# Where the modulation panels of a two-block transformer kernel are computed: fewer lent to GpSimd, more placed in the delta rule and the routing, and one square moved

## The chip, the cores and the metric

One Trainium2 chip, one of its cores. The metric is the device time of one launch in microseconds (us); lower is better. Engines are named as in the profile: PE is TensorE (PEld its weight loads), DVE VectorE, ACT ScalarE, POOL GpSimd, SP SyncE, which here only issues the transfers of weights.

## The reference

256 tokens of width 1024 go through two blocks, all in float32.

```python
# first block, two layers
h = h + mix(rmsnorm(h))              # layer 0: attention + pooling; layer 1: spatial gating + gated delta rule
h = h + memory_cross_attention(rmsnorm(h), mem_n, wq, wkv, wo)
h = h + conv_ffn(rmsnorm(h))
# second block, two layers
mod = silu(c) @ ada_w[l] + ada_b[l]  # 1024 x 6144, one row
sh_m, sc_m, g_m, sh_f, sc_f, g_f = split(mod, 6)
x = x + g_m * (four_attentions(rmsnorm(x) * (1 + sc_m) + sh_m) @ w_out[l])
x = x + g_f * ffn(rmsnorm(x) * (1 + sc_f) + sh_f)   # layer 0 swiglu, layer 1 eight experts, top 2
```

`c` is an input, so `mod` depends on nothing else that the kernel computes. One of the four attentions of the second block is the difference attention, whose output is normalised by head (`o * rsqrt(mean(o*o))`).

## The kernel before

Weights arrive as panels of 1 MB (128 x 2048 floats), in one fixed order, in a ring of six slots. SP loads panel n into slot n % 6 once panel n - 6 is released. All engines run their own program, written out by hand, and meet at semaphores; each does its instructions strictly in the order of the program.

The order of the stages, with the names in the code: mix0 (attention "moba", pooling, output projection), xat0 (first cross attention), ffn0, mix1 (spatial gating and delta rule), xat1 (second cross attention), ffn1, mix2 (attentions "s0"), ffn2, mix3 (attentions "s1"), ffn3 (routing, then the experts). Each stage begins with `transpose_norm`, in which PE turns the normalised tokens; before that PE has to wait for the norm on DVE and ACT.

The `mod` of both layers needs 48 panels of `ada_w` (2 layers x 6 parts x 4 quarters, `ADA_ORDER`). Each is done in one of two ways:

- **on PE, at a hook.** `ada(hook, n)` does n panels with eight matmuls of 128x256 each against the conditioning vector spread over 128 columns (`COND`), L1036. `ADA_AT` says how many at which hook; a hook with a stage's name stands at the start of `transpose_norm`. DVE reads the result in its own `ada(hook)`: a gate part (2 or 5) in one operation, L2258, the others in three, L2261 to L2267. 17 panels before.
- **lent to POOL.** For a name in `LENT_AHEAD` the panel of `ada_w` is put in the ring ahead of the named weight panel. POOL multiplies it by the conditioning vector and adds it up to 128x256 (`sum_lent`, L2664 to L2670), in one of three buffers `LENTS`; only then is the ring slot free. PE adds the 128 partitions with a few small matmuls (`take`, L577, or L574 for a gate part) and frees the buffer; DVE adds the result (`taken`, L2285 or L2282). POOL starts a stage's panels when that stage's norm is there, and panel i waits until panel i - 3 is taken. `TAKE_LATER` says after which step of a cross attention how many are taken and into which PSUM bank. 31 panels before: 2 in mix0 (taken in xat0), 10 in xat0, 11 in mix1, 8 in xat1.

A cross attention (`cross`) is: four query panels `xq`, in layer 0 the key panels `xk` 0 and 1 (7 us of PE each), then `attention`: step s computes the scores of unit s (four units), a panel `xv` beside it, the turned probabilities of unit s - 2 and the mixing of unit s - 3. Between scores and turned probabilities DVE scales the scores, finds the maxima (L1923, L1929), ACT takes the exponential (L1463) and DVE scales the result in place (L1941). The last steps, s = 4 to 6, have no panel beside them. Then follows `project`, four panels `xattn_wo`.

In mix1 PE inverts a matrix in five levels (`lv` 1 to 5) with one panel beside each, then scans four chunks; at the end it waits for DVE's last norm (`delta_out`) before `turn_outputs` and `project`.

In mix2 and mix3 the difference attention is the first of the four. `keep` on ACT copies the mixed result of a group out of PSUM (L1410) and, for the difference attention, squares it right after (L1517, `diff_squares`). PE uses the squares in `diff_sums` (L711), which stands after the whole `attention`; the scale that comes of them is needed at the last of the four output panels (`diff_spread`, L721).

In ffn3 PE computes the router's logits (L889), turns the tokens back (L897) while DVE picks the two best experts, then the places (L905), and gathers the first expert's tokens (L917) before the loop over the experts begins (L947).

Of the kernel before, what the change touches and what calls it, by code (L numbers as in the profile page):

```python
# [27 lines left out]
ACT = mybir.ActivationFunctionType  # L28
# [101 lines left out]
def build_program(nc, d, out):  # L130

    with ExitStack() as ctx:
# [34 lines left out]
        with ExitStack() as over_it:  # L167
# [5 lines left out]
            OT = under("OT", KD, T)  # L173
# [312 lines left out]
        def moe_unit(what, it, c):  # L486
# [9 lines left out]
        ADA_AT = {"xat0": 1, "ffn0": 1, "mix1": 1, "xat1": 1, "ffn1": 1, "mix2": 4,  # L496
                  "ffn2": 3, "mix3": 3, "ffn3": 2}

        LENT_AHEAD = {"mix0": (("out", "mix0", 0), ("out", "mix0", 2)),  # L500
                      "xat0": tuple(("xq", 0, j) for j in range(4)) + (("xk", 0, 0), ("xk", 0, 1)) + tuple(("xv", 0, j) for j in range(4)),
                      "mix1": tuple(("qkv", j) for j in range(6)) + (("u", 0), ("u", 1), ("vz", 0), ("vz", 1), ("gate", 0)),
# [3 lines left out]
        TAKE_LATER = {"xat0": {("xq", 1): (2, 4), ("xq", 3): (1, 5), ("xk", 0): (1, 6), ("xk", 1): (1, 7),  # L506
                               0: (1, 7), 1: (1, 6), 2: (1, 7), 3: (1, 6), 4: (1, 7), 5: (1, 6), 6: (1, 7)},
# [22 lines left out]
        def _(pe):  # L530
# [351 lines left out]
            def experts():  # L882
# [16 lines left out]

                ps = claim("places")  # L900
# [249 lines left out]
            for lv in range(1, len(LEVELS)):  # L1150
                if lv == 1:
                    panel_tok(("vz", 1))
                elif lv < 4:
                    panel_tok(("gate", lv - 2))
                else:
                    panel_T(("xk", 1, lv - 4), rhs=MT)
                if lv > 1:
                    take(("mix1", lv + 2), 1)
                pe.wait_ge(sem("level_ready"), lv)
                for tb in range(NT):  # L1160
                    products(("y", lv), M_of(gM), M_of(gX), tb)
                wait_read((("y", lv), 0), (("y", lv), 1))
                if lv < len(LEVELS) - 1:
                    for tb in range(NT):
                        products(("z", lv), M_of(gXT), M_of(gY), tb)
                for tb in range(NT):
                    products(("zt", lv), M_of(gY), M_of(gXT), tb)
                if lv == 4:
                    pe.wait_ge(sem("vn_ready"), 1)
                    for j in range(2):  # L1170
                        ps = claim(("sgu", j))
                        for c in range(2):
                            for tb in range(NT):
                                g = 2 * j + c
                                m = nc.tensor.matmul(ps[:, c * T + tb * P:c * T + tb * P + P],
                                                     VG[:, tb, g * P:g * P + P], WST[:, g, :], start=True, stop=True)
                        filled(m, ("sgu", j))
# [9 lines left out]
            for n in range(4):  # L1187
# [29 lines left out]
                filled(m, ("so", n))  # L1217
            pe.wait_ge(sem("delta_out"), 1)
# [188 lines left out]
        def _(act):  # L1407
# [98 lines left out]
            def keep(key, u):  # L1506
# [8 lines left out]
                if u["turns"] == 2:  # L1515
                    wait_drained(act, name)
                    nc.scalar.activation(DSQ, dst, ACT.Square).then_inc(sem("diff_squares"), 1)  # L1517
# [275 lines left out]
            for layer in range(2):  # L1793
# [39 lines left out]
                attention(k2)  # L1833
                act.wait_ge(sem("diff_mean"), layer + 1)
# [17 lines left out]
        def _(dve):  # L1852
# [272 lines left out]
            def experts():  # L2125
# [87 lines left out]
                tokens_low(0, base[2], base[3])  # L2213
                rounds = expert_rounds(dve)
# [220 lines left out]
            for lv in range(1, len(LEVELS)):  # L2435
# [41 lines left out]
                if lv > 1:  # L2477
                    taken(("mix1", lv + 2))
# [17 lines left out]
            for n in range(4):  # L2496
# [32 lines left out]
                .then_inc(sem("delta_out"), 1)  # L2529
            evac(("ot", "mix1", 1), OT[:, 6:8, :])  # L2530
# [108 lines left out]
        def _(pool):  # L2639
# [62 lines left out]
            sum_lent("mix0")  # L2702
# [220 lines left out]
```

## Time and profile before

| | us |
|---|---|
| median of 3 runs | 2716.41 (2714.31 to 2717.51) |
| the profiled execution, its own time | 2719.55 |
| its span in the profile, first to last instruction | 2717.7 |
| PE busy | 2619.8 (96%) |
| DVE busy | 1726.9 (64%) |
| ACT busy | 1309.5 (48%) |
| POOL busy | 301.7 (11%) |
| mean granted clock of TensorE | 0.984 of 2.4 GHz |

### The profile page before, as it was taken

To read this page: it belongs to the slowest core of one execution; us is meant where nothing else is said; L and a number is where in the kernel's file an instruction comes from. 1 tells how busy PE (TensorE), PEld (TensorE's weight loads), DVE (VectorE), ACT (ScalarE), POOL (GpSimd) and SP (SyncE) were. 2 spreads that over 40 slices of the span, in tenths; PEclk is the share of its full clock that TensorE was granted. 3 is DMA by queue.
4 is the path that set the end of the run, shared out by engine and by line. 5 is a ranking of instruction groups with operands and counts; after the bars stand their busy time and mean duration, and the time that the engine had idled before them with its cause. 6 is when DMAs were issued, how large, how long until landed. Compare 5 with 4: busy or idle time off the path is not lost.

```text
span 2717.7 us, 39002 instructions
## 1 busy us (share of the span) xinstructions
PE 2619.8 (96%) x13620; PEld 2171.0 (80%) x13620; DVE 1726.9 (64%) x2535; ACT 1309.5 (48%) x1931; POOL 301.7 (11%) x288
## 2 busy tenths in 40 slices
PE   7999999999899999999999998999999999999998
PEld 7677898887587998767998775888888888887886
DVE  1312776662226773555553553989898989889897
ACT  2211544411124442243332242777777777777776
POOL 0465000860360000000000000000000000000000
PEclk9999999999899999999999998999999999999999
DMA  7345544441355445315444303989898989898997
GB/s 318 124 182 214 209 185 160 186 179 68 135 205 194 186 185 180 106 35 201 186 185 164 107 33 118 359 322 383 319 381 328 375 329 374 322 366 336 349 365 277
DMA packets 87635, 627.29 MB, mean 231 GB/s; under 512 B 9760, under 2 KB 9920, under 8 KB 12800
## 3 DMA queue, kind: packets, MB, share of 16 engines
q1 hardware_dynamic: 84512, 613.45, 59.7%
q0 software_dynamic: 2480, 11.31, 1.1%
q8 instruction: 57, 0.93, 0.1%
q10 hardware_dynamic: 560, 1.38, 0.1%
q14 instruction: 26, 0.21, 0.0%
HBM read 625.06 MB, written 1.05 MB: 230 GB/s over the span
## 4 chain that ended last, share of the span: by engine, by line
PE 93%; DVE 3%; ACT 2%; issue 1%; POOL 1%; DMA 0%; DVEq 0%; SPq 0%; ACTq 0%; POOLq 0%
PE bank L947 23%; PE bank L838 14%; PE bank L975 11%; PE bank L606 11%; PE bank L852 7%; PE bank L619 6%; PE bank L791 6%; PE bank L655 2%; PE bank L693 2%; PE bank L1075 1%; PE bank L1036 1%; PE bank L990 1%; PE bank L917 1%; PE bank L962 1%; PE bank L679 1%
## 5 line engine op out<-in xcount | busy, mean ns | idle before, releaser
L1410 ACT ACTIVATE sb_parts<-sb_ring 128x1024 fp32r<-128x1024 f32 x873 | 873.0, 1053 | 125.0 <-PE bank L975 38.6
L2155 DVE TENSOR_TENSOR sb_parts<-sb_ring,sb_parts 128x1024 fp32r<-128x1024 f32 x675 | 786.9, 1218 | 10.8 <-ACT sb_parts L1410 10.8
L947 PE MATMUL bank<-sb_parts 128*128 128x512 f32 x2688 | 661.5, 396 | 2.5 <-DVE sb_parts L2147 1.8
L947 PEld LDWEIGHTS bank<-sb_parts 128*128 128x128 f32 x2688 | 494.9, 188 | 113.5 <-issue 9.4
L838 PE MATMUL bank<-sb_parts 128*128 128x256 f32 x3168 | 387.3, 284 | 7.1 <-DVE sb_XT L2080 5.8
L838 PEld LDWEIGHTS bank<-sb_parts 128*128 128x128 f32 x3168 | 386.1, 193 | 9.9 <-issue 7.7
L975 PE MATMUL bank<-sb_parts 128*128 128x512 f32 x1344 | 323.8, 390 | 0.0
L975 PEld LDWEIGHTS bank<-sb_parts 128*128 128x128 f32 x1344 | 251.7, 188 | 52.1
L606 PE MATMUL bank<-sb_XT,sb_ring 128*128 128x256 f32 x1152 | 259.7, 385 | 7.0 <-DVE sb_XT L1902 3.9
L2057 DVE TENSOR_TENSOR sb_parts<-sb_ring,sb_parts 128x1024 fp32r<-128x1024 f32 x198 | 232.8, 1220 | 34.3 <-ACT sb_parts L1410 34.3
L606 PEld LDWEIGHTS bank<-sb_XT,sb_ring 128*128 128x128 f32 x1152 | 219.6, 193 | 42.2 <-issue 12.7
L1410 ACT ACTIVATE sb_REG<-bank 128x512 f32<-128x512 f32 (+2 forms) x119 | 67.1, 574 | 338.7 <-PE bank L606 197.6
L852 PE MATMUL bank<-sb_parts 128*128 128x512 f32 x792 | 185.3, 390 | 0.0
L791 PE MATMUL bank<-sb_ring,sb_OT 128*128 128x512 f32 x384 | 168.9, 600 | 3.3 <-DVE sb_OT L1966 1.7
L852 PEld LDWEIGHTS bank<-sb_parts 128*128 128x128 f32 x792 | 146.6, 188 | 29.5 <-DVE sb_parts L2057 0.3
L2664 POOL TENSOR_TENSOR sb_ring<-sb_ring,sb_small 128x512 f32<-128x512 f32 x124 | 131.4, 1091 | 196.7 <-DVE sb_XH L1887 164.2
L791 PEld LDWEIGHTS bank<-sb_ring,sb_OT 128*128 128x128 f32 x384 | 73.2, 192 | 94.0 <-issue 90.9
L1463 ACT ACTIVATE sb_REG<-sb_REG,sb_small 128x256 f32<-128x256 f32 x112 | 56.0, 500 | 144.1 <-DVE sb_small L1929 144.1
L619 PE MATMUL bank<-sb_ring,sb_XT 128*128 128x256 f32 (+1 forms) x512 | 116.4, 389 | 4.2 <-ACT sb_O L1806 4.2
L619 PEld LDWEIGHTS bank<-sb_ring,sb_XT 128*128 128x128 f32 x512 | 98.3, 201 | 19.7 <-issue 6.6
L1410 ACT ACTIVATE sb_parts<-bank 128x256 fp32r<-128x256 f32 (+1 forms) x130 | 52.8, 413 | 121.7 <-PE bank L962 112.2
L1427 ACT ACTIVATE sb_XH<-sb_H 128x1024 f32<-128x1024 f32 x24 | 25.2, 1049 | 160.5 <-DVE sb_H L2030 100.2
(345 smaller groups left out, 2379.7 us busy)
## 6 DMA issues: line engine op xcount, KB each, us to landing
sb_ring<-in_moe_panels SPq DMA_DIRECT2D x342, 1024.0 KB, 4.9
sb_ring<-in_ada_w SPq DMA_DIRECT2D x48, 1024.0 KB, 4.8
sb_ring<-in_ffn_w_up SPq DMA_DIRECT2D x44, 1024.0 KB, 4.9
sb_ring<-in_ffn_w SPq DMA_DIRECT2D x33, 1024.0 KB, 4.8
sb_ring<-in_w_in SPq DMA_DIRECT2D x26, 1024.0 KB, 4.8
sb_ring<-in_ffn_w_down SPq DMA_DIRECT2D x22, 1024.0 KB, 6.6
sb_ring<-in_xattn_wkv SPq DMA_DIRECT2D x16, 1024.0 KB, 6.9
sb_ring<-in_od_w_in SPq DMA_DIRECT2D x12, 1024.0 KB, 5.6
```

The lines of the kernel that those rows point to most:

```text
L606: m = nc.tensor.matmul(ps[:, c * T:c * T + T], wt[:, k, c * P:c * P + P], rhs[:, k, :], start=k == 0, stop=k == KD - 1)
L619: m = nc.tensor.matmul(ps[:, tb * T:tb * T + w], lhs[:, k, tb * P:tb * P + P], wt[:, k, 0:w], start=k == 0, stop=k == KD - 1)
L791: m = nc.tensor.matmul(acc[j][:, :], OT[:, 2 * pair + c, j // 2 * P:j // 2 * P + P], wt[:, c, j % 2 * 512:j % 2 * 512 + 512], start=kk == ...
L838: m = nc.tensor.matmul(banks[b][:, half * T:half * T + T], w[:, kk, :], x[:, kk, :], start=t == 0, stop=t == len(terms) - 1)
L852: m = nc.tensor.matmul(banks[4 + j][:, :], h[:, g, tb], w[u][:, half], start=start and c == 0 and t == 0, stop=stop and c == 1 and t == 2, ...
L947: m = nc.tensor.matmul(banks[par][:, :], x[:, k, :], w[:, cols], start=k == 0 and t == 0, stop=k == KD - 1 and t == 2, skip_group_check=True)
L975: m = nc.tensor.matmul(banks[4 + j][:, :], h[:, par, c, :], w[:, cols], start=start and c == 0 and t == 0, stop=stop and c == 1 and t == 2 ...
L1410: return nc.scalar.activation(out, in_, ACT.Copy)
L1463: m = nc.scalar.activation(PR[:, g % 3, j, :], SS[:, g % 2, j, :], ACT.Exp, bias=NM[:, 2 * (g % 4) + j:2 * (g % 4) + j + 1], accum_out=RS[ ...
L2057: V_.tensor_tensor(as_panel(LOW[u], what), half_panel(n, what, c, it), as_panel(HIGH[u], what), ALU.subtract).then_inc(sem("low_ready"), 1)
L2155: V_.tensor_tensor(LOW[u], ring[slot][:, 1024 * c:1024 * c + 1024], HIGH[u], ALU.subtract) \
L2664: m = G.tensor_tensor(w[:, k:k + 2, :], w[:, k:k + 2, :], c[:, k:k + 2, :], ALU.mult)
```

## The change

It changes which of the 48 modulation panels are computed where, and where one square stands:

- `LENT_AHEAD`: the 2 lent panels of mix0 are gone, xat0 has 7 in place of 10, mix1 has 12 in place of 11. So 27 are lent, and 21 are done on PE.
- `TAKE_LATER["xat0"]`: 7 takes of one panel each, after `xq` 3, `xk` 0 and steps 0, 1, 3, 5, 6, in place of 12 panels taken after `xq` 1 (two), `xq` 3, `xk` 0, `xk` 1 and steps 0 to 6.
- mix1 takes one panel at every level, the first included.
- `ADA_AT`: a new hook "delta" with 2 panels, before PE's wait for `delta_out`; a new hook "route" with 3 panels, between the turned tokens and PE's wait for the chosen experts; ffn3 has 1 in place of 2.
- The square of the difference attention moves from the middle of ACT's attention to its end.

As `ADA_ORDER` is fixed, every hook and every take after the first works on other parts than before.

```diff
-        ADA_AT = {"xat0": 1, "ffn0": 1, "mix1": 1, "xat1": 1, "ffn1": 1, "mix2": 4,
-                  "ffn2": 3, "mix3": 3, "ffn3": 2}
+        ADA_AT = {"xat0": 1, "ffn0": 1, "mix1": 1, "delta": 2, "xat1": 1, "ffn1": 1, "mix2": 4,
+                  "ffn2": 3, "mix3": 3, "ffn3": 1, "route": 3}
-        LENT_AHEAD = {"mix0": (("out", "mix0", 0), ("out", "mix0", 2)),
-                      "xat0": tuple(("xq", 0, j) for j in range(4)) + (("xk", 0, 0), ("xk", 0, 1)) + tuple(("xv", 0, j) for j in range(4)),
-                      "mix1": tuple(("qkv", j) for j in range(6)) + (("u", 0), ("u", 1), ("vz", 0), ("vz", 1), ("gate", 0)),
+        LENT_AHEAD = {"xat0": (("xq", 0, 0), ("xq", 0, 1), ("xq", 0, 3), ("xk", 0, 0), ("xv", 0, 0), ("xv", 0, 1), ("xv", 0, 3)),
+                      "mix1": tuple(("qkv", j) for j in range(6)) + (("u", 0), ("u", 1), ("vz", 0), ("vz", 1), ("gate", 0), ("gate", 1)),
-        TAKE_LATER = {"xat0": {("xq", 1): (2, 4), ("xq", 3): (1, 5), ("xk", 0): (1, 6), ("xk", 1): (1, 7),
-                               0: (1, 7), 1: (1, 6), 2: (1, 7), 3: (1, 6), 4: (1, 7), 5: (1, 6), 6: (1, 7)},
+        TAKE_LATER = {"xat0": {("xq", 3): (1, 4), ("xk", 0): (1, 5), 0: (1, 7), 1: (1, 6), 3: (1, 6), 5: (1, 7), 6: (1, 6)},
...
# tensor, experts(), after the turned tokens
+                ada("route", ADA_AT["route"])
                 ps = claim("places")
                 pe.wait_ge(sem("experts_chosen"), 1)
...
# tensor, the levels of mix1 (vector: the same with taken)
-                if lv > 1:
-                    take(("mix1", lv + 2), 1)
+                take(("mix1", "lv", lv), 1)
...
# tensor, after the scan
+            ada("delta", ADA_AT["delta"])
             pe.wait_ge(sem("delta_out"), 1)
...
# scalar, keep()
-                if u["turns"] == 2:
-                    wait_drained(act, name)
-                    nc.scalar.activation(DSQ, dst, ACT.Square).then_inc(sem("diff_squares"), 1)
...
# scalar, mix2 and mix3
                 attention(k2)
+                wait_drained(act, ("mixed", k2, 0))
+                nc.scalar.activation(DSQ, OT[:, 0:2, :], ACT.Square).then_inc(sem("diff_squares"), 1)
...
# vector, experts(), after the first tokens_low
+                ada("route")
...
# vector, after delta_out
+            ada("delta")
             evac(("ot", "mix1", 1), OT[:, 6:8, :])
...
# gpsimd
-            sum_lent("mix0")
             sum_lent("xat0")
```

## Rows read from the trace of the kernel before

**Rows 1.** The page, busy time, share of the span and instructions, PE to POOL
```profile
PE 2619.8 (96%) x13620; PEld 2171.0 (80%) x13620; DVE 1726.9 (64%) x2535; ACT 1309.5 (48%) x1931; POOL 301.7 (11%) x288
```

**Rows 2.** Timeline, end of attention in mix0: start us, us, instruction [idle before]
```profile
102.86 1.13 PE L655 MATMUL bank<-sb_REG 64*128 64x256 f32 x4
102.88 2.36 DVE L1941 TENSOR_SCALAR sb_REG<-sb_REG,sb_small 128x256 f32<-128x256 f32 x2
...
105.39 0.63 PE L679 MATMUL bank<-sb_CST,sb_REG 128*128 128x128 f32 x4 [1.40 <-DVE sb_REG L1941]
...
112.70 1.99 PE L1059 MATMUL bank<-sb_REG 128*128 128x256 f32 x8
```

**Rows 3.** Timeline, end of the attentions in mix2, PE, DVE and ACT
```profile
1198.23 1.13 PE L655 MATMUL bank<-sb_REG 64*128 64x256 f32 x4
1198.26 0.61 DVE L1941 TENSOR_SCALAR sb_REG<-sb_REG,sb_small 128x256 f32<-128x256 f32 x2
...
1205.85 1.95 PE L711 MATMUL bank<-sb_CST,sb_XH 128*128 128x1 f32 x16
1205.96 0.60 ACT L1410 ACTIVATE sb_OT<-bank 128x512 f32<-128x512 f32 x1 [1.18 <-PE bank L693]
...
1207.66 4.54 PE L791 MATMUL bank<-sb_ring,sb_OT 128*128 128x512 f32 x10
```

**Rows 4.** Timeline of PE in the first cross attention
```profile
165.22 14.06 PE L606 MATMUL bank<-sb_XT,sb_ring 128*128 128x256 f32 x64
...
181.52 8.74 PE L606 MATMUL bank<-sb_MT,sb_ring 128*128 128x256 f32 x32 [1.90 <-DMA sb_ring<-in_xattn_wkv]
...
207.52 0.50 PE L577 MATMUL bank<-sb_CST,sb_LENTS 128*128 128x1 f32 x4
...
241.53 0.63 PE L679 MATMUL bank<-sb_CST,sb_REG 128*128 128x128 f32 x4 [0.87 <-DVE sb_REG L1941]
...
247.16 0.58 PE L577 MATMUL bank<-sb_CST,sb_LENTS 128*128 128x1 f32 x4 [0.99 <-POOL sb_LENTS L2670]
```

**Rows 5.** Timeline of POOL there: the last operation of two lent panels in succession
```profile
173.54 0.72 POOL L2670 TENSOR_TENSOR sb_LENTS<-sb_ring 128x256 f32<-128x256 f32 x1
...
182.24 0.72 POOL L2670 TENSOR_TENSOR sb_LENTS<-sb_ring 128x256 f32<-128x256 f32 x1
```

**Rows 6.** Timeline of PE at the end of the delta rule
```profile
686.17 1.97 PE L769 MATMUL bank<-sb_CST,sb_O 128*128 128x128 f32 x8 [7.49 <-DVE sb_O L2528]
688.97 16.55 PE L791 MATMUL bank<-sb_ring,sb_OT 128*128 128x512 f32 x33 [0.83 <-issue]
...
718.67 3.62 PE L1036 MATMUL bank<-sb_ring,sb_COND 128*128 128x256 f32 x16
```

**Rows 7.** Windows: stretch, us, busy PE, PEld, DVE, ACT, POOL, granted clock, DMA share, GB/s
```profile
686.10:693.00 6.90, 6.00 (x13) 3.42 (x14) 0.71 (x2) 0.60 (x1) 0.00 (x0) 0.50 0.00 0
...
1669.50:1690.00 20.50, 15.26 (x72) 14.82 (x72) 10.50 (x39) 5.70 (x9) 0.00 (x0) 0.50 0.04 9
```

**Rows 8.** Timeline of ACT in the attentions of mix2, the square
```profile
1181.77 0.63 ACT L1517 ACTIVATE sb_XH<-sb_OT 128x512 f32<-128x512 f32 x1
```

**Rows 9.** Timeline of PE, with one row of DVE, from the norm of ffn3 to the experts' loop
```profile
1657.44 7.07 PE L1036 MATMUL bank<-sb_ring,sb_COND 128*128 128x256 f32 x32
1665.03 1.97 PE L633 MATMUL bank<-sb_CST,sb_XH 128*128 128x128 f32 x16 [0.51 <-DVE sb_XH L1887]
...
1668.05 0.75 DVE L2258 TENSOR_TENSOR sb_GATE<-bank,sb_GATE 128x256 f32<-128x256 f32 x2
...
1674.38 3.65 PE L897 MATMUL bank<-sb_CST,sb_XT 128*128 128x128 f32 x16
1679.77 2.27 PE L905 MATMUL bank<-sb_REG,sb_CST 128*128 128x9 f32 x10 [1.73 <-DVE sb_REG L2631]
1685.55 5.93 PE L917 MATMUL bank<-sb_REG,sb_XH 128*128 128x128 f32 x32 [3.51 <-DVE sb_REG L2137]
1693.25 3.03 PE L947 MATMUL bank<-sb_parts 128*128 128x512 f32 x12 [1.77 <-DVE sb_parts L2147]
```

More of the change, by code:

```diff
@@ L2476, in _ @@
                         step(V_.tensor_tensor(u_, tmp, u_, ALU.mult))
-                if lv > 1:
-                    taken(("mix1", lv + 2))
+                taken(("mix1", "lv", lv))
                 evac((("y", lv), 1), flat(gY)[:, 512:1024], bank_of((("y", lv), 1))[:, :])
```

## The prediction, made before the changed kernel was run

> **What bounds the kernel now.** I read the page first. PE is busy for 2619.8 us of a span of 2717.7, so it sets the time almost everywhere [rows 1]. A change can then do three things: give PE less or more to do, fill or open one of its waits (97.9 us in all), or move its granted clock, whose mean is 0.984. The list of PE's waits says where the waits are, and the largest single one behind something other than a norm at a stage's start is that at the end of the delta rule. Then I read the timeline at each place that the diff touches, and there the reader is to look at the gap in brackets and at the duration of the row behind it: a row twice as long as its like ran at 1.2 GHz. The windows say so directly [rows 7]. The experts' loop, the last 1020 us, is not touched and has no waits of PE; it only starts earlier or later.
>
> **Prices.** A modulation panel on PE costs 3.62 us as one and 7.07 as two in a row, so about 3.6 each [rows 6, 9]. A lent one costs PE a take, a row of 0.50 of which the next matmul overlaps some: 0.4 [rows 4]. POOL needs 8.7 us for it (182.24 less 173.54) [rows 5]. Four panels more on PE are thus 14.4 us of work, against 1.6 of takes saved. Everything hangs on which waits they fall into.
>
> **End of attention in mix0.** The two lent panels go. POOL summed the second one beside DVE's scaling L1941, which took 2.36 us for two, where the same pair takes 0.61 with POOL idle [rows 2, 3]. PE waits 1.40 for it and then runs some rows at half clock. From the last scores to the end of the mixing it is 112.70 - 102.86 = 9.84 us here, and 1205.85 - 1198.23 = 7.62 in mix2, where the same steps run without POOL [rows 2, 3]. I take the whole difference: -2.2 (bounds 0, if the two stages differ for another reason, and -2.4). The Trainium skill (SBUF — State Buffer, SBUF: two separate sides) says that VectorE and GpSimd take turns at a shared pair of ports, each for a whole instruction; by that rule the wait goes with POOL's work, which the trace bears out with 2.36 against 0.61.
>
> **First cross attention (xat0).** Five takes fewer are 2.0, of which one after `xk` 1 now covers a wait for the same panel's copy: -1.6. The wait of 1.90 for the weights of `xk` 0 is one for a ring slot that POOL held: before, it had two panels of mix0 to be taken first and then four in five panels. A weight panel is 14.06 / 2 = 7.03 us of PE [rows 4], so POOL at 8.7 fell behind. In the new order there is no lent panel before `xq` 2 and only one between `xq` 3 and `xk` 1, and POOL's third is done at 173.4, before PE reaches the first take: -1.9. The panel behind that wait took 8.74, where its like take 7.0 to 7.15, at half clock in part: -1.6. Then POOL: its fourth panel starts with the take at 178.7, the last of its seven ends near 221, while PE has 20 us of steps left. So the last steps have no POOL beside them; the wait of 0.87 for L1941 goes (2.36 becomes 0.61) and the 0.99 for the last `LENTS` too [rows 4]: -1.9. Laid out step by step PE reaches the output projection near 240.6, and 248.0 before. Sum -7.0, by the layout -7.4; I take -7.2 (bounds -4.5, if the takes and the DVE wait give nothing, and -8). The ring is late nowhere: the longest hold is the fourth lent panel until 187.8, and the panel loaded in its slot (`xv` 1) is wanted at 205.
>
> **mix1, levels.** One take more on PE at level 1, where PE did not wait: +0.4. POOL's twelfth panel runs in levels 1 and 2 beside DVE: 0 to +1.1 more. +0.4.
>
> **Delta rule.** Two panels, 7.07 to 7.24, go into a wait of 7.49 [rows 6], so they are done just before `delta_out`. DVE adds them behind that (0.75 for two, [rows 9]) while PE turns the outputs: nothing. If DVE were late there, it would be by 0.8. More comes from the clock: after the wait PE ran at half until 693.0 [rows 7]; 8 transposes took 1.97, where 16 take the same in ffn3 [rows 6, 9], so 1.0 is lost there, and of 4.0 us of projection half, 2.0. With PE busy all the way the clock has no reason to fall: -3.0 (bounds 0, if the panels do not hold it, and -3.3).
>
> **The square.** In the middle of ACT's attention nobody waited for it (0.63, [rows 8]) and PE had no gap there, so taking it away gives 0. At the end PE waits: before, L711 started at 1205.85; now ACT first copies the last group (until 1206.56), then squares for 0.63, and L711 starts at 1207.3 [rows 3, 8]. The projection is behind L711 in PE's program, though its first panel needs nothing of it. +1.45 in mix2 and in mix3, 2.9. A new gap can also bring the clock down; if it does, that costs up to 3.0 each (6.9 us at 0.50 with 6.0 busy, [rows 7]). I take +0.5 each on average: +3.9 (bounds 2.9 and 8.9).
>
> **ffn3 and the routing.** Before, two panels (7.07) covered the norm but for 0.51 [rows 9]. One of them leaves a wait of 4.0: no gain, and with the half clock beginning a little earlier +0.8. The three panels stand between the turned tokens, which end at 1678.0, and a wait of 1.73. They are 10.7, and the clock is at half there (1669.5 to 1690.0, [rows 7]), so some 1.2 more until it rises. Behind them all is in series: places, DVE's slots (3.51), gather, split (1.77), and nothing of it can start earlier. Given back: the wait of 1.73; the places, 2.27 at half clock, 1.1; the gather, 5.93, of which a clock at full would give back 2.3, but the wait of 3.51 comes before it: 1.4. Sum 0.8 + 10.7 + 1.2 - 1.7 - 1.1 - 1.4 = +8.5 (bounds +6, all at full clock, and +12, nothing given back). The ring has the experts' first three panels by then, and the other three come before the gather ends.
>
> The Trainium skill (TensorE: Matmul & The Clock Gate, Part 1: The HAM clock gate) says that half rate is the default and activity lifts it. By that rule the three panels would lift it before the places, the lower bound of +6; it also speaks against the 4.0 us left open before the transposes of ffn3 and against the square's gap.
>
> **Sum.** -2.2 - 7.2 + 0.4 - 3.0 + 3.9 + 8.5 = +0.4. The profiled execution took 2719.55 by its own time (1.85 more than its span), 3.1 above the median of 2716.41. So 2719.95 for a like execution, and 2716.8 as a median. What a measurement can tell from no change is some 0.2%, 5.4 us: faster is below 2711.0, slower above 2721.8.
>
> **The rivals.**
> - *The routing is cheap.* The panels lift the clock within the first of them and it stays: +6 there, and the square opens no clock loss, +2.9. Then -2.2 - 7.4 + 0.4 - 3.0 + 2.9 + 6 = -3.3, and with one of the half-clock stretches elsewhere falling away (3.0, as above) -6.3: 2710. For: 15.26 busy in 20.5 us at half is 7.6 lost, a large sum to win back. Against: the wait of 3.51 stays. Chance 0.25, half of which is past the bound.
> - *Slower: the clock falls at the new gaps.* The 4.0 in ffn3, the 3.5 before the gather and the two squares' gaps lie between gaps after which rows ran at half (7.49 and 1.90 did it, [rows 4, 6]) and those that left the clock alone (0.51, [rows 9]). Routing +11, squares +6: sum +5.0 or more, 2722. It decides once the squares and the gather all run at half. Chance 0.2.
> - *Spacing does nothing.* POOL is as late as before, as its wait is for the takes: xat0 gives only the five takes and the part in mix0, so +0.4 + 5.6 = +6.0, 2722. Against: the layout leaves POOL 20 us. Chance 0.05.
> - *The panels in the delta rule are late* (a slot is not loaded): +3.6 there, 2720, within the forecast.
>
> **How the numbers follow.** The forecast, 2711 to 2722, has 0.5 of the chance. The range for 8 in 10 adds the most of the first two rivals: 2709 to 2723. Faster: 0.12 from the first rival and 0.13 from a forecast whose routing or square I have too dear: 0.25. Slower: 0.2. Same: 0.55.
>
> **What would show it.** PE's wait at L769 under 0.5 and the granted clock at 1.00 over 680 to 705; no DMA wait in xat0 and its projection 9 to 10 us earlier than before (with mix0's part); L711 with a wait of 1.4 behind ACT's square; three panels at L1036 in the routing and the experts' loop starting some 8 later after the norm of ffn3 than before. It is wrong if the places do not wait for the panels, if POOL is still late in xat0, or if the clock's stretches at half outside these places change by more than two.

## The result, and the profile after

| | before | after |
|---|---|---|
| median of the runs | 2717.49 (2714.31 to 2719.84, 8 runs) | 2724.34 (2721.96 to 2726.92, 8 runs) |
| ratio, 95% interval | | 1.0024 [1.0013, 1.0035] |
| span of the profiled execution | 2717.7 | 2722.7 |
| PE busy; mean granted clock | 2619.8; 0.984 | 2631.9; 0.986 |

The change makes the kernel slower: by the medians 6.85 us, by the ratio 6.5 (3.5 to 9.5), where the forecast was +0.4. At 2724.34 it lies 2 us above the upper rival's place (2722) and 1.3 above the range's end of 2723. Of the 7.5 us between the forecast of 2716.8 and the result, 1.1 is the kernel before, whose median was 2716.41 in the three runs at hand then and 2717.49 in eight. The experts' loop takes 1024.5 us to the end in both profiles, so all of it is decided ahead of it.

The page of the kernel after, first part; its line answers to [rows 1]: 12 us more of PE and 32 POOL instructions fewer (the 4 panels).

```profile
PE 2631.9 (97%) x13680; PEld 2182.4 (80%) x13680; DVE 1720.3 (63%) x2531; ACT 1308.7 (48%) x1931; POOL 267.9 (10%) x256
```

Timeline of the kernel after, end of attention in mix0, PE and DVE. It answers to [rows 2]: the scaling takes 0.62 where it took 2.36, PE's wait of 1.40 is one of 0.72, and from the last scores to the end of the mixing it is 112.52 - 104.79 = 7.73 in place of 9.84.

```profile
104.79 1.13 PE L653 MATMUL bank<-sb_REG 64*128 64x256 f32 x4
...
107.48 0.61 DVE L1939 TENSOR_SCALAR sb_REG<-sb_REG,sb_small 128x256 f32<-128x256 f32 x2
108.24 0.63 PE L677 MATMUL bank<-sb_CST,sb_REG 128*128 128x128 f32 x4 [0.72 <-DVE sb_REG L1939]
...
112.52 1.99 PE L1058 MATMUL bank<-sb_REG 128*128 128x256 f32 x8
```

Timeline of PE after, first cross attention. It answers to [rows 4]: both key panels take 7.15, no row waits for a transfer, and the output projection starts 240.09 - 147.08 = 93.01 behind the norm's transposes, where it was 248.03 - 147.25 = 100.78. One wait has grown, from 0.86 to 1.20, ahead of the scores of the first step; in this whole stage the granted clock is 1.00 (windows 180 to 194, 194 to 200 and 200 to 240). It will matter for the lesson.

```profile
185.74 7.15 PE L604 MATMUL bank<-sb_MT,sb_ring 128*128 128x256 f32 x32
...
194.09 1.96 PE L653 MATMUL bank<-sb_REG 128*128 128x256 f32 x8 [1.20 <-DVE sb_REG L1862]
...
240.09 2.41 PE L789 MATMUL bank<-sb_ring,sb_OT 128*128 128x512 f32 x5 [0.25 <-DVE sb_MODC L2284]
```

Timeline of DVE in the same stage, all four pairs of the scaling. POOL's last operation there ends at 221.33: the two pairs that it worked beside took 2.28 each, the two after it 0.62.

```profile
206.69 2.28 DVE L1939 TENSOR_SCALAR sb_REG<-sb_REG,sb_small 128x256 f32<-128x256 f32 x2
215.77 2.28 DVE L1939 TENSOR_SCALAR sb_REG<-sb_REG,sb_small 128x256 f32<-128x256 f32 x2
224.84 0.62 DVE L1939 TENSOR_SCALAR sb_REG<-sb_REG,sb_small 128x256 f32<-128x256 f32 x2
233.66 0.62 DVE L1939 TENSOR_SCALAR sb_REG<-sb_REG,sb_small 128x256 f32<-128x256 f32 x2
```

Timeline of PE after, from the last chunks of the levels to the end of the delta rule's projection. It answers to [rows 6]: the two panels stand where the wait of 7.49 was, and the projection takes 27.70, where it took 29.86. Its first row is new: a wait for a PSUM bank, of which more below.

```profile
639.23 7.14 PE L604 MATMUL bank<-sb_MT,sb_ring 128*128 128x256 f32 x32 [0.87 <-DVE sb_REG L1862]
...
672.55 8.36 PE L1035 MATMUL bank<-sb_ring,sb_COND 128*128 128x256 f32 x32
680.75 1.04 PE L767 MATMUL bank<-sb_CST,sb_O 128*128 128x128 f32 x8
682.62 27.70 PE L789 MATMUL bank<-sb_ring,sb_OT 128*128 128x512 f32 x64 [0.83 <-DVE sb_OT L1862]
710.16 3.62 PE L1035 MATMUL bank<-sb_ring,sb_COND 128*128 128x256 f32 x16
```

Timeline of PE and ACT after, the square's new place in mix2. It answers to [rows 3, 8]: ACT's copy ends at 1198.14, the square follows, and PE stands for 1.20. The 48 rows behind it take 22.54.

```profile
1198.04 0.62 ACT L1831 ACTIVATE sb_XH<-sb_OT 128x512 f32<-128x512 f32 x1
1198.71 1.95 PE L709 MATMUL bank<-sb_CST,sb_XH 128*128 128x1 f32 x16 [1.20 <-ACT sb_XH L1831]
1200.52 22.54 PE L789 MATMUL bank<-sb_ring,sb_OT 128*128 128x512 f32 x48
1222.90 1.05 PE L719 MATMUL bank<-sb_CST,sb_XH 128*128 128x128 f32 x8
```

Timeline of PE after, from the norm of ffn3 to the experts' loop. It answers to [rows 9], and a reader should add up from the first row to the last: 1698.20 - 1651.73 = 46.47, where it was 1693.25 - 1657.44 = 35.81.

```profile
1651.73 3.62 PE L1035 MATMUL bank<-sb_ring,sb_COND 128*128 128x256 f32 x16
1659.32 3.68 PE L631 MATMUL bank<-sb_CST,sb_XH 128*128 128x128 f32 x16 [3.97 <-DVE sb_XH L1885]
1664.39 6.96 PE L887 MATMUL bank<-sb_WR,sb_XT 128*128 128x8 f32 x32 [1.40 <-DVE sb_XT L1903]
1671.21 3.65 PE L895 MATMUL bank<-sb_CST,sb_XT 128*128 128x128 f32 x16
1674.65 10.75 PE L1035 MATMUL bank<-sb_ring,sb_COND 128*128 128x256 f32 x48
1685.24 1.18 PE L904 MATMUL bank<-sb_REG,sb_CST 128*128 128x9 f32 x10
1689.93 6.50 PE L916 MATMUL bank<-sb_REG,sb_XH 128*128 128x128 f32 x32 [3.51 <-DVE sb_REG L2135]
1698.20 3.01 PE L946 MATMUL bank<-sb_parts 128*128 128x512 f32 x12 [1.77 <-DVE sb_parts L2145]
```

Windows of the kernel after (columns as in [rows 7]), for the projection behind the delta rule, behind the square, and before, on and behind the three panels. The granted clock is full at the first, mostly half at the second, half up to the panels, full on them and at half again on the gather.

```profile
682.60:689.50 6.90, 6.88 (x16) 3.14 (x17) 0.00 (x0) 0.00 (x0) 0.00 (x0) 1.00 0.32 132
...
1200.50:1204.50 4.00, 4.00 (x8) 1.70 (x8) 1.02 (x5) 0.21 (x1) 0.00 (x0) 0.57 0.00 0
1658.00:1675.00 17.00, 14.29 (x65) 13.91 (x66) 6.54 (x26) 5.10 (x10) 0.00 (x0) 0.50 0.17 68
1675.00:1689.00 14.00, 11.42 (x58) 10.03 (x56) 3.42 (x17) 3.33 (x4) 0.00 (x0) 0.99 0.56 205
1689.00:1696.00 7.00, 6.07 (x30) 6.10 (x31) 4.87 (x8) 0.60 (x1) 0.00 (x0) 0.53 0.46 163
```

The difference by step, each from one PE row to the next in both profiles:

| step | predicted | profiles |
|---|---|---|
| the first 45 us, which the change does not touch | 0 | +1.9 |
| end of attention in mix0 | -2.2 | -2.1 |
| first cross attention | -7.2 | -7.8 |
| mix1, norm to the end of the scan | +0.4 | +1.8 |
| end of the scan to the end of the projection | -3.0 | -2.4 |
| square: wait in both stages | +2.9 | 1.4 + 1.2 |
| square: half clock in both projections | +1.0 | 1.7 + 1.7 |
| ffn3 and routing | +8.5 | +10.7 |
| half-clock stretches inside mix3 and ffn2 | 0 | -3.2 |
| sum at the experts' loop | +0.4 | +4.9 |

Those 1.9 at the start are not the change's: PE's second row of transposes begins between 43.55 and 46.08 in the fourteen profiles of this case, at 45.11 in the one in which only the square was moved (e4). The profile of before is the lowest of them. The last row but one is not the change's either, as far as can be seen. The rows that an edit touches add up to +6.2, the row of the stretches takes 3.2 of that, and the medians differ by 6.85.

How far can such a table be trusted? Each column is one execution, and half-clock stretches move between executions. e1, e2 and the changed kernel run the same instructions in mix1, and from its norm to that of xat1 their profiles show 246.70, 244.99 and 247.66 us. Mix2, with the same instructions in the changed kernel, e2, e3, e7, e10 and e12, takes 210.9 to 214.6. So a stage's difference of under some 3 us in one pair of profiles can be such a stretch, and the medians decide.

### The profile page after: what moved, and what is told of

Read it like the earlier page. It is cut to its first block, busy times and chain, and to the rows that moved or that the text cites. A ratio compares the mean times of both kernels' runs of the same rounds, so it can differ in the third digit from the quotient of the medians.

```text
span 2722.7 us, 39079 instructions
## 1 busy us (share of the span) xinstructions
PE 2631.9 (97%) x13680; PEld 2182.4 (80%) x13680; DVE 1720.3 (63%) x2531; ACT 1308.7 (48%) x1931; POOL 267.9 (10%) x256
## 4 chain that ended last, share of the span: by engine, by line
PE 94%; DVE 3%; ACT 2%; issue 1%; DMA 0%; DVEq 0%; SPq 0%; ACTq 0%
PE bank L946 23%; PE bank L836 14%; PE bank L604 12%; PE bank L974 11%; PE bank L850 7%; PE bank L789 6%; PE bank L617 6%; PE bank L653 2%; PE bank L691 2%; PE bank L1035 2%; PE bank L1074 1%; PE bank L916 1%; PE bank L989 1%; PE bank L961 1%; PE bank L677 1%
## 5 line engine op out<-in xcount | busy, mean ns | idle before, releaser
L2663 POOL TENSOR_TENSOR sb_ring<-sb_ring,sb_small 128x512 f32<-128x512 f32 x108 | 114.8, 1093 | 203.0 <-DVE sb_XH L1885 179.0
```

What stands on the lines that cost most here:

```text
L2663: m = G.tensor_tensor(w[:, k:k + 2, :], w[:, k:k + 2, :], c[:, k:k + 2, :], ALU.mult)
```

## The experiments

Each ratio is against runs of the kernel before made with it, whose median was 2717.87 (for e1, e2, e3, e5), 2718.3 (e4, e6 to e8) and 2718.69 (e9 to e12). Differences in us are worked out from the ratios; each ratio is known to some 2.5 us either way, those of e9 to e11 to some 3.8.

**e6, the changed kernel again.** No edit.

> The changed kernel once more, for a second profile of it. If the half clock in a place is of that place's gaps, it is there in this profile too; if the place only met it by the moment, it isn't. Expected the same 6.6 us over the kernel before, the half clock again at the start of ffn3 and at the gather, and in one or both of the projections of mix2 and mix3; the stretches in the middle of mix1, mix2 and mix3 some other than in the first profile. The first four weight panels took 29.7 us in the first profile and 27.9 in that of the kernel before, with nothing changed there: either may be seen.

2724.25, ratio 1.002 [1.001, 1.003]. The starts of the stages in its profile lie within 0.1 us of the first profile's, and its half-clock stretches too. Not every execution is like these two: the spans of e6 go from 2720.0 to 2725.4 us and the mean granted clock from 0.986 to 0.988. So a stretch at half clock can be blamed on an edit only where it comes and goes with the edit in many profiles. Below, "against the changed kernel" is against this ratio.

**e1, the square back in the middle of the attention.**

```diff
# the changed kernel, keep() on ACT
+                if u["turns"] == 2:
+                    wait_drained(act, name)
+                    nc.scalar.activation(DSQ, dst, ACT.Square).then_inc(sem("diff_squares"), 1)
# behind attention(k2)
-                wait_drained(act, ("mixed", k2, 0))
-                nc.scalar.activation(DSQ, OT[:, 0:2, :], ACT.Square).then_inc(sem("diff_squares"), 1)
```

> The changed kernel with the square back in the middle of ACT's attention; all else stays. Theory 1 (the late square costs a wait and, by the gap, clock): the changed kernel has a wait of 1.20 us ahead of the head sums in mix2 and in mix3, and behind each the output projection takes 22.5 us for 48 rows where 20.85 is its time at full clock. Both go: 2 x (1.2 + 1.7) = 5.8 us less than the changed kernel, so about 1 us over the kernel before. Rival (only the wait is the square's doing, the half clock falls there by chance): 2.4 less, and a projection of over 22 us is still seen in one of the two layers. Rival 2 (ACT is slowed in its attention and PE waits there instead): no gain.

2718.64, ratio 0.9997 [0.9988, 1.0006], 6.3 less than the changed kernel. The timeline of PE shows the sums right behind the mixing, with no wait:

```profile
1198.15 1.84 PE L691 MATMUL bank<-sb_REG 128*64 128x128 f32 x16
1199.92 1.95 PE L709 MATMUL bank<-sb_CST,sb_XH 128*128 128x1 f32 x16
1201.73 13.55 PE L789 MATMUL bank<-sb_ring,sb_OT 128*128 128x512 f32 x31
```

Putting the square back is enough to bring the change from "slower" to "no difference" (moving the panels of the routing, e2 below, is enough too). The profile shows less of it: mix2 and mix3 together, norm to norm, are 2.4 shorter, as rows elsewhere in these two stages ran at half clock that did not in the changed kernel's profile.

**e4, the other side: the kernel before with only the square moved** (the edit of e1 the other way round, on the kernel before).

> The kernel before with the square moved to the end of ACT's attention and nothing else changed. Theory 1: a wait of 1.2 us in mix2 and in mix3 and some half clock in the projection behind it: 2.4 to 5.8 us slower than the kernel before, 5 by my guess. Rival (the half clock there came from other parts of the change): exactly the wait, 2.4, and projections of 20.9 us.

2721.57, ratio 1.0014 [1.0005, 1.0023]: +3.8. Two windows of it, at the start of the projections of mix2 and mix3:

```profile
1210.00:1214.00 4.00, 4.00 (x10) 2.20 (x10) 1.03 (x5) 0.21 (x1) 0.00 (x0) 0.57 0.00 0
1630.00:1634.00 4.00, 4.00 (x9) 2.06 (x9) 1.03 (x5) 0.21 (x1) 0.00 (x0) 0.57 0.02 4
```

The half clock comes with the square in a kernel that has nothing else of the change. Its local cost in this profile is 1.4 + 1.5 in mix2 (169.49 against 168.08 from norm to projection, 41.40 against 39.91 from there to the next norm), and 1.5 behind it in mix3; inside mix3 and ffn3 fewer rows than before run at half, which gives part of it back, so that mix2 and mix3 together are 2.3 longer than before. The routing, with the instructions of before, takes 33.67 from the end of the projection to the loop, where the profile of before has 35.81: the places run at full clock in e4 (1.25) and at half there (2.27).

**e5, the gap filled instead: the sums between the first and the second output panel.** ACT squares where the change has it.

```diff
                 attention(k2)
-                diff_sums(k2)
...
-                        {0: lambda: diff_spread(k2)})
+                        {1: lambda: diff_sums(k2), 0: lambda: diff_spread(k2)})
```

> The changed kernel with the head sums of the difference attention (one column each) moved on PE behind the first output panel, whose data doesn't need them; the square stays at the end of ACT's attention. Theory 1 (PE only waits because the sums stand ahead of the projection in its program): the wait of 1.2 us goes in both layers, and with no gap ahead of the projection its clock holds: 5.8 less than the changed kernel, as with the square put back. Rival (the scale is then late at the last output panel): a wait ahead of the spreading of the scale, of some us, and less gain.

2718.06, ratio 1.0001 [0.9992, 1.001]. PE goes from the mixing into the first panel and finds the squares done:

```profile
1197.87 1.84 PE L691 MATMUL bank<-sb_REG 128*64 128x128 f32 x16
1199.65 7.13 PE L789 MATMUL bank<-sb_ring,sb_OT 128*128 128x512 f32 x16
1206.62 1.84 PE L709 MATMUL bank<-sb_CST,sb_XH 128*128 128x1 f32 x16
```

So it is PE's wait that costs, with the clock behind it, and not where ACT squares. It gives 5.2 us, e1 gave 6.3; with these intervals the two are the same.

**e2, the three panels of the routing put into ffn3's hook.**

```diff
-                  "ffn2": 3, "mix3": 3, "ffn3": 1, "route": 3}
+                  "ffn2": 3, "mix3": 3, "ffn3": 4, "route": 0}
```

> The changed kernel with the three panels of the routing put back at the start of ffn3, which then has four. Theory 1 (behind the turned tokens the panels are bare, at the start of ffn3 the norm hides two of them): from the end of the last projection to the experts' loop the changed kernel takes 46.5 us (1651.7 to 1698.2), the kernel before 35.8. Four panels are 14.2, the norm needs 7.6, so 6.6 stand bare: 35.8 + 6.6 = 42.4, and the wait of 4.0 with the half clock over the transposes goes. So 4 us less than the changed kernel. Rival (the clock is what the routing's panels pay for): with no panels there the router to the gather runs at half throughout as before, and the whole is as long as in the changed kernel.

2716.55, ratio 0.9999 [0.999, 1.0008]. From the end of the projection to the loop it is 1689.88 - 1649.49 = 40.39, and 46.47 in the changed kernel: three panels behind the turned tokens are 6 us dearer than the same three in front of a norm, where the first of them fills the wait of 3.97 and the clock stays up until the router. It is still 4.6 more than before, for two panels more.

**e7, one panel behind the places, in the wait for DVE's slots, and three at ffn3.** Of the two waits in the routing, the change filled the short one (1.73); the long one (3.51) is behind the places.

```diff
-                  "ffn2": 3, "mix3": 3, "ffn3": 1, "route": 3}
+                  "ffn2": 3, "mix3": 3, "ffn3": 3, "route": 0, "places": 1}
# tensor, experts(), after the places' matmuls
                 filled(m, "places")
+                ada("places", ADA_AT["places"])
# vector, experts()
                 ada("route")
+                ada("places")
```

> The changed kernel with three panels at the start of ffn3 and one behind the matmuls of the places, where PE waits 3.5 us for DVE's slots; none ahead of the places. Theory 1 (a panel costs nothing where PE waits at least as long, and all its time elsewhere): three panels, 10.6, less the norm's 7.6, leave 3.0 bare, the fourth is hidden in the wait of 3.5 and lifts the clock for the gather (5.9 to 6.5 at half, 3.6 to 4 at full). So from the last projection to the experts' loop 35.8 + 3.0 - 2 = 37 us against 46.5: 9 less than the changed kernel, and 2 to 3 under the kernel before. Rival (the clock at the gather does not rise with one panel): 7 less.

2713.29, ratio 0.998 [0.9971, 0.9989]: 11 less than the changed kernel, and faster than before. The timeline of PE:

```profile
1677.94 2.27 PE L904 MATMUL bank<-sb_REG,sb_CST 128*128 128x9 f32 x10 [1.73 <-DVE sb_REG L2632]
1680.06 6.12 PE L1036 MATMUL bank<-sb_ring,sb_COND 128*128 128x256 f32 x16
1686.02 3.73 PE L917 MATMUL bank<-sb_REG,sb_XH 128*128 128x128 f32 x32
```

The panel stands where the wait was, and the gather behind it runs at full clock, 3.73 against 6.50 and, before, 5.93. The panel begins at half clock and is longer than the wait: from the places to the gather it is 8.08 where it was 5.78 before, and from the gather to the loop 5.50 where it was 7.70, so the panel cost 0.1 in all. From the end of the projection it is 36.92 to the loop, 9.6 less than the changed kernel.

**e3, the turn of the banks in mix1 as before.** The extra take at level 1 shifts which PSUM bank each later product gets.

```diff
                 take(("mix1", "lv", lv), 1)
+                if lv == 1:
+                    aside[0] += 3
```

> The changed kernel, with the turn of the PSUM banks 4 to 7 set back after the take of level 1, so that all later products of mix1 stand in the same banks as in the kernel before. Theory 1 (the one take more shifts the turn by one, the key panel 2, which is put in bank 4 by name, then waits for a copy out of that bank by DVE): the wait of 0.87 us ahead of that panel, which the kernel before doesn't have, goes; 0.9 less, or 2.5 if the clock then holds to the end of the scan too. Rival (the wait is of DVE being later through the take): the wait stays.

2723.29, ratio 1.0021 [1.0012, 1.003]: no gain. The wait of 0.87 at the second key panel is gone, and another stands at level 1:

```profile
569.59 2.02 PE L1074 MATMUL bank<-sb_REG 128*128 128x128 f32 x16 [1.04 <-DVE sb_MODC L2286]
```

The take's bank is now wanted before DVE, in order behind other work, has read it. Theory 1 falls for the median: with this order of turns the take at level 1 costs a wait at one place or the other.

A second thing is seen in mix1 when e2's profile is read beside the changed kernel's, whose instructions are the same there. e2 has the same wait, 0.88, but the scan ends at full clock, and the panels behind it take 7.17 in place of 8.36:

```profile
671.05 7.17 PE L1035 MATMUL bank<-sb_ring,sb_COND 128*128 128x256 f32 x32
678.61 1.09 PE L767 MATMUL bank<-sb_CST,sb_O 128*128 128x128 f32 x8 [0.39 <-DVE sb_O L2526]
```

From the norm to the end of the scan it is 202.70 there, 204.79 in the changed kernel and 202.93 before; from there to the end of the projection 37.03, 37.61 and 40.06.

**e8, everything into waits:** the square as in e1, the banks as in e3, two panels at ffn3, one behind the places, and one behind the transposes of ffn2, where PE waits 5.8 for the first activations.

```diff
+                  "ffn2": 3, "split0": 1, "mix3": 3, "ffn3": 2, "route": 0, "places": 1}
...
                 transpose_norm(f"ffn{2 + layer}")
+                ada(f"split{layer}", ADA_AT.get(f"split{layer}", 0))
```

> The changed kernel with the square back, the banks of mix1 as before, no panel ahead of the places, and the 21 panels of PE so placed that each lies in a wait: two at the start of ffn3, one behind the places, three at the start of ffn2 and one more behind its transposes, where PE waits 5.8 us for the split tokens. Theory 1, by the terms read: end of attention in mix0 -2.1, first cross attention -7.75, mix1 +0.4, delta rule -2.4 to -4, ffn2 0 to -1, ffn3 as in the kernel before 0, gather -2. So 14 to 16 under the kernel before. Rival (the freed time is lost to the clock or to DVE, which has one more panel to add ahead of its first work in ffn2): under 8.

2713.46, ratio 0.9976 [0.9967, 0.9986]. The routing did as expected (34.16 to the loop), the panel in ffn2 did not:

```profile
1250.65 5.88 PE L1036 MATMUL bank<-sb_ring,sb_COND 128*128 128x256 f32 x16 [6.96 <-DVE sb_SPREAD L2267]
1256.19 6.09 PE L836 MATMUL bank<-sb_parts 128*128 128x256 f32 x48
```

It waited for the bank of the hook's first panel, which DVE reads only after it has split the activations, so it sat behind the wait it was to fill. The whole gave 6.5 us against the kernel before, where 14 to 16 were expected. 211.75 from this norm to the next, 207.3 in the changed kernel.

**e9, the same panel in another bank,** without e3's turn.

```diff
-                ada(f"split{layer}", ADA_AT.get(f"split{layer}", 0))
+                ada(f"split{layer}", ADA_AT.get(f"split{layer}", 0), 7, 1)
```

> As e8, but the panel that stands behind the transposes of ffn2 is written to PSUM bank 7, which no panel of the hook holds, and without the three banks of e3, which gave nothing. Theory 1 (the panel of e8 was late because its bank was held, not because there is no room): it starts right behind the transposes, fills the 5.85 us in which PE waits for the first activations of ffn2 (3.6 of them), and from the norm of ffn2 to that of mix3 it is 207 to 208 us in place of 211.75. e8's 2713.5 less 4.4 is 2709, ratio to the kernel before 0.9966. Theory 2 (a panel there costs its 3.6 wherever its bank is, since DVE's reading of it delays the activations): 211 us again, 2713.

2703.07 (2700.15 to 2708.31), ratio 0.9945 [0.9931, 0.9959]: 15 less than before, the fastest of all. The timeline of PE:

```profile
1241.57 1.93 PE L631 MATMUL bank<-sb_CST,sb_XH 128*128 128x128 f32 x16
1243.33 3.62 PE L1036 MATMUL bank<-sb_ring,sb_COND 128*128 128x256 f32 x16
1249.34 2.87 PE L836 MATMUL bank<-sb_parts 128*128 128x256 f32 x22 [2.39 <-issue]
```

Norm to norm is now 1446.57 - 1241.57 = 205.0, less than in the changed kernel, which has a panel less there. The windows of both say why, e9 first and the changed kernel second:

```profile
1243.00:1256.00 13.00, 10.61 (x76) 9.88 (x75) 12.24 (x26) 6.78 (x12) 0.00 (x0) 1.00 0.41 155
```
```profile
1243.00:1256.00 13.00, 7.15 (x41) 6.94 (x40) 11.50 (x23) 6.68 (x11) 0.00 (x0) 0.74 0.29 90
```

Over half of the wait is filled, and the rows behind it run at full clock. The other difference from e8, the turn of the banks, is not what did it: mix1 takes 246.67 here and 246.73 in e8.

**e11, e7 and e1 together.**

> Two changes to the changed kernel, each tried alone before: three panels at ffn3, none in front of the wait for the chosen experts and one behind the places (e7), and the square back in the middle of the attention (e1). Theory 1 (both losses are local and add up): 2724.3 - 11.0 - 5.8 = 2707.5, ratio 0.996; no half clock in the projections of mix2 and mix3. Theory 2 (part of what either gave was half-clock stretches that fall elsewhere, as e8 leaves open): 2711 to 2713, ratio 0.998.

2707.51, ratio 0.9962 [0.9949, 0.9976]: the two losses add up. That it meets the 2707.5 of theory 1 so closely is luck, as the interval is 7 us wide. Against e7's profile mix2 and mix3 are 9.75 shorter, more than the 5.8 that the square takes on the spot; the rest is half-clock stretches again.

**e10, the delta rule's panels in front of the norm of xat1.**

```diff
-"mix1": 1, "delta": 2, "xat1": 1,
+"mix1": 1, "delta": 0, "xat1": 3,
```

> The changed kernel with the two panels of the delta rule put in front of the norm of xat1 (three there in place of one). Theory 1 (the two panels are hidden in PE's wait for the last norm of the delta rule and hold the clock): the wait of 7.5 comes back with rows at half clock behind it, 2.4 us from the end of the scan to the end of the projection, and in xat1 7.1 us of panels stand against the 1.6 in which PE waits for the norm: +5.5. Sum +7.9 against the changed kernel's 2724.3: 2732, ratio 1.0052. Theory 2 (the panels in the delta rule delay something of their own, so taking them out gives back): under 2729.

2734.14, ratio 1.0053 [1.0039, 1.0067], 9 more than the changed kernel. The old wait and the slow rows are back:

```profile
679.54 1.97 PE L767 MATMUL bank<-sb_CST,sb_O 128*128 128x128 f32 x8 [7.49 <-DVE sb_O L2526]
682.34 30.61 PE L789 MATMUL bank<-sb_ring,sb_OT 128*128 128x512 f32 x64 [0.83 <-issue]
712.78 10.52 PE L1035 MATMUL bank<-sb_ring,sb_COND 128*128 128x256 f32 x48
723.14 1.91 PE L631 MATMUL bank<-sb_CST,sb_XH 128*128 128x128 f32 x16
```

Norm of mix1 to the end of the projection is 245.17 against 242.40 (+2.8), and from there to the transposes 10.36 against 5.26 (+5.1). The rest, 1.8, is one half-clock stretch more in mix2, where nothing was edited.

**e12, the same seven lent panels in the first cross attention, packed together instead of spaced.**

```diff
-"xat0": (("xq", 0, 0), ("xq", 0, 1), ("xq", 0, 3), ("xk", 0, 0), ("xv", 0, 0), ("xv", 0, 1), ("xv", 0, 3))
+"xat0": (("xq", 0, 0), ("xq", 0, 1), ("xq", 0, 2), ("xq", 0, 3), ("xk", 0, 0), ("xk", 0, 1), ("xv", 0, 0))
```

> The changed kernel with its seven lent panels of the first cross attention in front of seven neighbouring weight panels (xq 0 to 3, xk 0 and 1, xv 0) in place of spaced out; the takes stay where they are. Theory 1 (what gave 7.75 us is that there are fewer and that they are taken at later steps; a slot is held only until POOL has summed, and by that the last panel, xv 3, is free to load at 211.5 and wanted at 223.1): PE's rows in this stage stay as they are, 2724, ratio 1.002. Theory 2 (it is the spacing in the ring that counts, a lent panel in front of each weight panel holds the slots): a wait for a weight panel of 1.9 and half clock behind it, 3.5 in all, comes back: 2728, ratio 1.0035.

2724.47, ratio 1.0023 [1.0014, 1.0032]. 240.35 - 147.34 = 93.01 from norm to projection, as in the changed kernel to the hundredth. POOL's last operations end at the same distances too. The spacing in the ring gives nothing. What is left is that there are fewer panels and that they are taken at later steps; which of the two it is, no run separates.

## Why the prediction was wrong, step by step

The signs of all steps came out as forecast in these profiles. Two terms were mis-sized, the square (+6.0 for +3.9) and the routing (+10.7 for +8.5), and in both what was too small is the clock behind a gap.

**End of attention in mix0, and the first cross attention: right** (-2.1 for -2.2, -7.8 for -7.2). With POOL idle the scaling takes 0.62; the wait for the weights, the half clock behind it, the last steps' waits and five takes are gone. What was wrong is only the picture of the ring: the layout without neighbours was not needed (e12). That POOL's work lengthens DVE's is shown twice, by 2.36 against 0.62 for the same pair before and after the panels of mix0 went, and inside one stage of the changed kernel by 2.28 against 0.62, as POOL stops.

**mix1: +1.8 for +0.4.** The take was priced as a row. It also moves the turn of the banks, and 0.87 of waiting comes of that; the shift of banks is shown to move the wait (e3), at no gain. The rest is half clock, in the last rows of the scan (0.58 and 0.69 for rows that take 0.43) among others, and it is not shown to be the change's: in e2's profile, with the same instructions and the same wait, the way to the end of the scan is 0.2 shorter than before. So the two profiles put this term at +1.8 and at -0.2.

**Delta rule: right** (-2.4 for -3.0). PE's wait is gone and the clock holds through the projection. The panels took 8.36 where 7.07 to 7.24 was reckoned, since they began at half; in e2, where they did not, they took 7.17 and the term is exactly the -3.0 of the forecast. e10 prices them from the other side: without them there, +7.9 on the spot.

**The square: +6.0 for +3.9; this term was mis-sized.** The wait is 1.20 where I had 1.45. The step that failed is "I take +0.5 each on average" for the clock: every profile that has the wait has rows at half clock at both projections, 1.7 us each time, and neither the kernel before nor any of the five without the wait (e1, e5, e8, e9, e11) has any there. The eight profiles with it take 24.2 from the sums to the spreading of the scale, those without 22.5 (e5, which has the sums elsewhere, aside). Moved back it gives 6.3 (e1), moved alone it costs 3.8 (e4), taken out of PE's way it gives 5.2 (e5).

**ffn3 and the routing: +10.7 for +8.5; the other mis-sized term.** Step by step: the panels were 10.6, as reckoned, and at full clock, so the +1.2 on them fell away. The half clock that starts at the new wait of 3.97 cost 2.5 where I had 0.8 (transposes 3.68 against 1.97, router 6.96 against 6.04). The places and the wait before them gave 3.0 back, as reckoned 2.8. The step that failed worst is the gather's "-1.4": it was +0.6. The panels had lifted the clock, and the wait of 3.51 behind them let it fall again before the gather, 6.50 against 5.93. I had said that this wait stays, and still gave half the gain. Part of the baseline is one execution's: in e4's profile the routing of before is 2.1 shorter, and against that the term is +12.8. The Trainium skill (TensorE: Matmul & The Clock Gate, Part 1: The HAM clock gate) has the clock rise with activity and fall without it; the trace agrees with both halves, 0.99 on the panels and 0.53 on the gather, and I had given the second too little weight.

**The rivals.** "The clock falls at the new gaps" is what happened, at its own conditions (squares and gather at half) and nearly its prices: +11 and +6, against 10.7 and 6.0. I gave it 0.2. Its sum, 2722, took the mix1 term as +0.4 and stood on the lower median of the kernel before. That it ends so near is in part luck: the stretches away from the edits took 3.2 off the profile. "Routing cheap" fell with the gather, "spacing does nothing" with xat0, "late panels" with the absent wait at L767.

**Stays open.** Where rows fall to half clock away from any edit differs between kernels and between executions of one (in mix3 and ffn2 together 3.2 us less after than before); why, no run shows. Nor does any run show why the wait of 1.20 in the first cross attention left the clock at full and the one ahead of the sums did not. The medians differ by 1.9 more than the profiles, of which the profiled execution of the kernel before, 2.1 above its median, can be the reason. And e9 gained 10 over e8 in the medians where the profiles' spans show 7.8.

## What to carry over

Filler work is worth what it covers: three panels of 3.6 in front of a wait of 1.73 gave back 1.9 of their 10.6, and one in a wait of 3.51 (e7) or 5.85 (e9) cost nothing or less, because rows behind it then ran at full clock. So list PE's waits by length with the rows behind them, put the filler into the longest, and give it a bank that no engine still holds behind the very work PE waits for. And price a new gap on PE with the clock behind it as well as without: ahead of the square's sums 1.2 us of wait cost 2.9 on the spot, in eight profiles of eight, while a wait of the same 1.20 in the first cross attention cost no clock at all. The length of the gap alone does not tell the two apart, so the sum needs both prices and a chance between them.

## What the runs showed of the hardware

- Two profiles of the changed kernel agree to within 0.1 us over 2.7 ms, half-clock stretches included. Its other executions do not all (mean granted clock 0.986 to 0.988), and with the same instructions mix1 took 244.99, 246.70 or 247.66 in three kernels. The first 45 us vary by 2.5 us.
- A wait of 1.20 on PE with 128x1 matmuls behind it brought rows at half clock each time. A wait of 1.20 with scores of 128x256 behind it (changed kernel at 194.09) did not, nor did the two waits of 1.64 and 1.28 at the start of xat1; waits of 0.83 to 0.87 in the delta rule's projection and the levels did not, nor did 1.73 in front of the places when the clock was already at half, where it could do no more harm.
- A pair of DVE's scalings of 128x256 took 2.28 while POOL summed lent panels and 0.62 once POOL had stopped, in one stage.
- The clock rose on modulation panels in ffn3 and fell again within a wait of 3.51 behind them.
